# Eight of the attention output projection's products moved into the attention loop, with two accumulator banks held open

## What is computed

```python
q, k, v = jnp.split(h @ w_qkv, 3, axis=-1)          # h: 256 x 1024, 8 heads of 128
q = rotary(rms_norm(q, q_gain), pos)
k = rotary(rms_norm(k, k_gain), pos)
o = moba_attention(q, k, v)                          # one block of 256: causal softmax attention
x = x + o.reshape(B, S, D) @ w_o                     # the output projection
h = rms_norm(x, mlp_norm[l])
x = x + jnp.square(jax.nn.relu(h @ w_up[l])) @ w_down[l]
```

## Time and profile before

| | us |
|---|---|
| median of 3 runs | 1520.42 |
| lowest, highest | 1520.36, 1522.64 |
| the profiled execution, its own time | 1521.56 |
| its span | 1519.8 |
| mean granted TensorE clock | 0.911 |
| TensorE busy | 1236.7 (81%) |
| VectorE busy | 620.0 (41%) |
| ScalarE busy | 442.2 (29%) |

### The profile page before, as it was taken

How to read it: one execution, slowest core, us unless ns; L and a number is a source line. 1 busy time by engine, 2 the same in 40 slices (tenths; PEclk the granted TensorE clock), 3 DMA queues, 4 the chain that set the end, 5 groups by cost and what they waited for, 6 DMA issues and landing times.

```text
span 1519.8 us, 18140 instructions
## 1 busy us (share of the span) xinstructions
PE 1236.7 (81%) x7680; PEld 908.8 (60%) x7680; DVE 620.0 (41%) x999; ACT 442.2 (29%) x669; POOL 16.1 (1%) x32
## 2 busy tenths in 40 slices
PE   5998998999999998899999988488746646636647
PEld 5998785499887687599888677355312212212213
DVE  4687323377443565466643546943101101001002
ACT  4652330253332575353433412243000000000001
POOL 2000000000000000000000000000000000000000
PEclk9999999899999999999999988699877868878778
DMA  8353359255455554144454633046899999999996
GB/s 272 123 204 111 125 209 332 84 180 188 166 175 185 174 179 166 56 166 167 170 218 140 213 99 119 0 184 260 361 427 428 430 428 429 429 428 429 427 426 247
DMA packets 98059, 362.97 MB, mean 239 GB/s; under 512 B 7193, under 2 KB 10612, under 8 KB 86084
## 3 DMA queue, kind: packets, MB, share of 16 engines
q1 hardware_dynamic: 95952, 357.70, 60.8%
q0 software_dynamic: 1680, 4.10, 1.0%
q10 hardware_dynamic: 356, 0.13, 0.1%
HBM read 360.87 MB, written 1.05 MB: 238 GB/s over the span
## 4 chain that ended last, share of the span: by engine, by line
PE 59%; DMA 21%; DVE 8%; ACT 2%; issue 2%; SPq 1%; DVEq 0%; ACTq 0%
PE bank L856 31%; DMA arena<-in_exp_w 20%; PE bank L629 7%; PE bank L945 4%; PE bank L828 3%; PE bank L797 2%; PE bank L1463 2%; PE bank L838 2%; PE bank L1149 1%; PE bank L1110 1%; PE bank L1141 1%; DMA ring<-in_ple_gate 1%; SPq L2587 1%; DVE low_w L1571 1%; DVE arena L1968 1%
## 5 line engine op out<-in xcount | busy, mean ns | idle before, releaser
L629 PE MATMUL bank<-arena 128*32 128x512 f32 x944 | 199.2, 715 | 96.7 <-DMA arena<-in_exp_w 95.2
L1571 DVE TENSOR_TENSOR low_w<-ring,split_high 128x2048 fp32r<-128x2048 f32 x84 | 189.6, 2289 | 161.2 <-ACT split_high L2237 161.2
L856 PE MATMUL bank<-turned_high,low_w 128*128 128x256 f32 x720 | 204.7, 284 | 0.0
L2237 ACT ACTIVATE split_high<-ring 128x2048 fp32r<-128x2048 f32 x84 | 157.5, 1912 | 147.6 <-DMA ring<-in_w_down 59.3
L629 PE MATMUL bank<-ring,arena 128*32 128x512 f32 x528 | 92.2, 683 | 80.5 <-DMA arena<-in_exp_w 80.5
L2222 ACT ACTIVATE arena<-bank 128x512 f32<-128x512 f32 (+1 forms) x143 | 80.9, 593 | 248.7 <-PE bank L856 134.3
L629 PEld LDWEIGHTS bank<-arena 128*32 128x32 f32 x944 | 52.1, 129 | 168.8 <-issue 168.8
L856 PE MATMUL bank<-turned_high,split_high 128*128 128x256 f32 x512 | 145.4, 284 | 0.0
L856 PE MATMUL bank<-turned_low,split_high 128*128 128x256 f32 x512 | 144.9, 283 | 0.0
L856 PEld LDWEIGHTS bank<-turned_high,low_w 128*128 128x128 f32 x720 | 139.2, 193 | 0.0
L734 DVE TENSOR_TENSOR arena<-arena,bank 128x512 f32<-128x512 f32 x8 | 5.5, 688 | 290.1 <-PE bank L629 290.1
(11 more groups left out here) (427 smaller groups left out, 1978.3 us busy)
## 6 DMA issues: line engine op xcount, KB each, us to landing
arena<-in_exp_w SPq DMA_DIRECT2D x59, 2048.0 KB, 23.1
ring<-in_exp_w SPq DMA_DIRECT2D x33, 2048.0 KB, 20.4
ring<-in_w_up SPq DMA_DIRECT2D x16, 2048.0 KB, 8.6
ring<-in_w_down SPq DMA_DIRECT2D x16, 2048.0 KB, 7.8
ring<-in_mod_w SPq DMA_DIRECT2D x12, 2048.0 KB, 8.1
ring<-in_w_in_ar SPq DMA_DIRECT2D x7, 2048.0 KB, 8.5
ring<-in_w_qkv SPq DMA_DIRECT2D x6, 2048.0 KB, 8.6
ring<-in_ple_gate SPq DMA_DIRECT2D x4, 2048.0 KB, 7.9
```

The source lines that it names most:

```text
L629: last = mm(mb[bank][strip(e), :], act[:, k, strip(e)], w[e][:, k, cols], start=(k == 0), stop=(k == n_k - 1), skip_group_check=True)
L856: last = mm(dst, *pair, start=(start and i == 0), stop=(stop and i == 2))
L1571: v.tensor_tensor(low_of(name, s), half_of(slot(name), name, s), high_of(name, s).bitcast(F32), ALU.subtract).then_inc(sem("split_low"), 1)
L2237: nc.scalar.activation(high_of(name, s), half_of(slot(name), name, s), ACT.Copy)\
```

## The change

Inside the loop, behind the work of the items i2 = 7 to 14, one product of the projection is made each: k = (i2 - 7) // 2, t = (i2 - 7) % 2, for n = 0. Before each of them TensorE waits until the "o" of that chunk has been copied. The banks of (0,0) and (0,1) are held while they are open (from i2 = 7 and 8), so the loop has six banks in rotation from there. After the loop come chunks 4 and 5 of both, then the wait for the last copies, then chunks 6 and 7 of both, then (1,0) whole and four chunks of (1,1). With its last product a held piece is released. The other engines' programs are as before.

```diff
             def out_piece(tag, n, t, ks):
 
                 if ks[0] == 0:
-                    open_out[(tag, n, t)] = banks.take(pe, tag, n, t)
+                    open_out[(tag, n, t)] = (banks.hold if len(ks) == 1 else banks.take)(pe, tag, n, t)
                 bank = open_out[(tag, n, t)]
...
                 if ks[-1] == KC - 1:
                     last.then_inc(bank.full, 1)
+                    if (tag, n, t) in banks.held:
+                        banks.release(tag, n, t)
                     if t == NT - 1:
                         read_by(bank, tag, n)
...
-            def attend(tag, items_q, items_k, value, landed_sem, probs, probsT):
+            def attend(tag, items_q, items_k, value, landed_sem, probs, probsT, between=None):
...
                         if t == 1 and h >= 1:
                             out_of(tag, h - 1, value, probsT)
+                        if between:
+                            between(i2)
                 out_of(tag, HEADS - 1, value, probsT)
...
+            def one_product(i2):
+                if i2 < 7:
+                    return
+                k, t = divmod(i2 - 7, NT)
+                banks.wait_read(pe, "att", "o", k // 2)
+                if k < 4:
+                    out_piece("w_o", 0, t, [k])
+
             attend("att", lambda h: qT[:, h, :], lambda h: kT[:, h, :],
-                   lambda h, k: v_att[:, k, h * P:(h + 1) * P], "att_prob", prob, probT)
+                   lambda h, k: v_att[:, k, h * P:(h + 1) * P], "att_prob", prob, probT, one_product)
+            for t in range(NT):
+                out_piece("w_o", 0, t, range(4, 6))
             for c in range(4):
                 banks.wait_read(pe, "att", "o", c)
-            for n, t in ((0, 0), (0, 1), (1, 0)):
-                out_piece("w_o", n, t, range(KC))
+            for t in range(NT):
+                out_piece("w_o", 0, t, range(6, KC))
+            out_piece("w_o", 1, 0, range(KC))
             out_piece("w_o", 1, 1, range(4))
```

## The result

The changed kernel takes **1529.06 us** (median of 5 runs, 1527.36 to 1530.42) against 1520.36 us (1519.59 to 1522.64) of the kernel before beside it: ratio 1.0052, 95% interval 1.0039 to 1.0066. It is slower by 0.4 to 0.7%, inside the forecast range and on the forecast side. The profiled execution took 1528.75 us, its span is 1527.0 us, 7.2 more than before, with a mean clock of 0.906 (0.911 before).

A forecast was written before the change was run, and what follows sets the result against it. TensorE was taken to bound the kernel, through the projection behind layer 1's attention. A delay of 3.6 us plus 2.7 us of half clock gave 6.3 us over the median of 1520.42: 1526.7 us, range 1523.0 to 1530.0.

The forecast's parts named there:

- The loop: Layer 1's attention loop: with products inside and six banks, it ends 5.6 us later, including a 0.62 us bank wait.
- The new wait: Before (1,0): it gets the bank of (0,1) and waits for VectorE's addition, leaving TensorE idle for 6.2 us.
- 3.6 us without the clock: At the transposes behind the projection: 3.6 us later (648.97 against 645.35), before any half clock is added.
- The clock, 2.7 us: In the products behind the idle gap: half clock costs 2.7 us, bounds nothing to 5.7 us.
- The first rival: At the wait before (1,0): the wait comes but the clock stays, 1524.0 us; chance 0.16.
- What the change wins or loses up to the transposes moves the rest with it.: Behind the projection: any difference at the transposes (645.35 us before) passes on unchanged to the end.
- The second rival: Behind the transposes: VectorE, ScalarE or a weight load absorbs the delay later, 1520.4 us; chance 0.10.
- The third rival (faster): At (1,0): no wait for the bank of (0,1), so 2.6 us less, 1517.8 us; chance 0.06.
- The sum: Whole kernel: 3.6 us of delay plus 2.7 us of half clock, 6.3 us slower, 1526.7 us.
- the place: From the attention loop through the projection to the transposes of x: 6.3 us later, half clock included.

The follow-up runs named there:

- late_release: The changed kernel with both held banks released only after (1,1) is opened; 1520.76 us against 1521.51 of the kernel before, ratio 0.9991.
- early_split: The changed kernel, but ScalarE splits layer 1's first feed-forward weights without waiting for (0,0); 1522.80 us, ratio 1.0008 to the kernel before.
- fill_wait: The changed kernel with seven dummy products of zeros ahead of (1,0); 1527.29 us, ratio 1.0036 to the kernel before.
- shift1: The kernel before with one dummy product of zeros between (0,1) and (1,0); 3.3 us over before, ratio 1.0018.
- shift4: The kernel before with four dummy products of zeros between (0,1) and (1,0); 4.1 us over before, ratio 1.0029.

## Why the prediction was right, point by point

- **The loop.** Predicted: TensorE stands before transpose 10 at 616.55 and waits for the copy of "o" 1 until 617.17; the last head is issued at 625.54. Measured, less the 0.18 us of the common point: the copy ends at 617.11, the last head is issued at 624.46 + 1.34 - 0.18 = 625.62. The bank wait was foreseen at 0.62 us, the row has 0.45.
- **The new wait.** ScalarE's split predicted at 630.96, measured 630.98; the additions end predicted 638.60, measured 638.61; (1,0) predicted 638.65, measured 638.66. The idle of 6.2 us is 6.01 in the row. late_release and early_split showed that it is this bank and this chain.
- **3.6 us without the clock.** fill_wait has 3.72.
- **The clock, 2.7 us.** Taken from 56 records of layer 0. Measured 2.20 by the 24 records, 2.11 by fill_wait: the term was 0.5 too large, inside its bounds of 0 and 5.7. The half clock lasted less long among the products: in layer 0 from 268.73 to 274.1 us, here from 638.84 to about 643.1 (0.50 in 642 to 643 us, 0.93 in 643 to 644). The layer 0 products also stand behind a second wait of 4.04 us, which the prediction left out when it called the two places alike. The first rival (no fall) was wrong here. The rule of the Trainium skill (TensorE: Matmul & The Clock Gate, Why this matters for your kernels), by which idle gaps between bursts bring half clock, held for this gap. For the later waits of 2.66 and 3.3 to 3.7 us the traces show half clock behind some and full clock behind others, so there the measurements decide.
- **"What the change wins or loses up to the transposes moves the rest with it."** This step was incomplete. 5.83 us at the transposes became 7.0 in the profile and 8.7 between the medians (6 to 10 by the ratio's interval). The second rival had the sign wrong: nothing was absorbed, something was added. I read the earlier trace rows, a wait of 3.61 us with the clock at 1.00, as a property of that wait. It holds for that execution only: in the profile of shift1 a wait of 3.45 us there is followed by half clock.
- **The third rival (faster).** The gain of 2.6 us was real, and its condition too: late_release meets it with another bank and has 2.55.
- **The sum.** 6.3 us forecast; the two errors, -0.5 in the clock and +1.2 behind the place (in the profile; more between the medians), went opposite ways. The place is predicted well (6.3 us forecast, 5.8 measured), for the reasons given. The total is 8.7 us between the medians, and what lies behind the transposes had no term; that 1529.06 is still inside 1523.0 to 1530.0, by 0.9 us, is in part luck.

## What to carry to other kernels

Releasing a held accumulator with its last product gives its bank back to the rotation before anyone has read it, and if the rotation stands just ahead of it, the very next take gets it: look at which bank that take gets and who still has to read it. Here the place of two releases was worth 8.4 us at the transposes (31.65 us with the late release, 40.03 with the early one), while six banks instead of eight cost 0.8 there. When a kernel has several idle stretches of TensorE of some microseconds, judge a small edit by its own stretch in the trace and not by the total alone: a delay of 0.8 us (shift1) came with 3.3 us between the medians. To compare versions, fill those waits with dummy products first, and do not take the clock of one profiled execution for that of the kernel.

## What the runs showed of the hardware that I had not expected

- After the same wait of 2.66 us ahead of the same products the granted clock was 1.00 in 746 to 750 us (before) and in 748 to 752 us (shift4), and 0.57 in 752 to 756 us (after), 0.72 in 746 to 750 us (shift1). The idle time alone does not decide, and neither does the time since the start: before and shift1 start these products 0.11 us apart.
- The falls follow no order in the delay, in one profile each: 1 dummy product, both falls (78.11; 1.94 and 7.40 us); 2, both (78.06; 1.94 and 8.66); 4, none (76.48; 1.07 and 6.87); 7, only the second (76.47; 1.94 and 8.98).
- A fall need not come while the engine is idle. In shift1 TensorE resumes at 746.71 us, the granted clock is 1.00 in 746 to 747 us and 0.89 in 747 to 748, then 0.50. Its price varies: 1.35 us in after, 1.6 in most, 2.85 in early_split, where the same 336 records take 79.33 us and the clock is 0.50 from 744 to 748 us.
- Products of zeros keep the clock at 1.00 through a wait (fill_wait, 6 us of them) and cost nothing where they end before the wait does; in layer 0's gate, where 2.13 us of idle and eight small products came behind them, the clock still fell to 0.50.
